# A two-direction chunked scan on four quarters of the TensorE array, with work handed from VectorE and SyncE to GpSimd and ScalarE

## The reference, cut to what matters

```python
def wkv7_scan(r, logw, k, v, a, b, reverse):
    """S_t = S_{t-1} diag(exp(-exp(logw_t))) + (S_{t-1} a_t) b_t^T + v_t k_t^T ;  y_t = S_t r_t"""
    def step(S, inp):
        r_t, w_t, k_t, v_t, a_t, b_t = inp
        sa = jnp.einsum('bhij,bhj->bhi', S, a_t)
        S = (S * w_t[:, :, None, :] + sa[..., :, None] * b_t[..., None, :]
             + v_t[..., :, None] * k_t[..., None, :])
        return S, jnp.einsum('bhij,bhj->bhi', S, r_t)
...
for d, rev in ((0, False), (1, True)):
    wkv = wkv + wkv7_scan(heads(r), heads(logw[:, :, d]), heads(k_d), heads(v),
                          -kk, kk * heads(a_d), rev)
...
c = layer_norm(conv(c) + dw_bias)      # conformer branch, 512 channels
```

## Time and profile before

| what | us |
|---|---|
| median of 3 runs | 2501.82 (2499.22 to 2515.18) |
| profiled execution, its own time | 2509.72 |
| its span, first to last instruction | 2508.0 |
| scan, first level product to the last but four steps | 804.0 to 1112.1: 19 steps |
| last four steps and the end of the scan | 1112.1 to about 1180 |

### The profile page before, as it was taken

One profiled execution on the slowest core, in us unless ns is written; L12 is line 12 of the kernel. 1 busy time (PEld: TensorE's weight loads), 2 busy tenths in 40 slices (PEclk: granted clock), 3 DMA queues, 4 the chain that ended last, 5 costly groups with the idle time before them and its releaser, 6 DMA issues. The chain is left out here.

```text
span 2508.0 us, 50080 instructions
## 1 busy us (share of the span) xinstructions
PE 2328.4 (93%) x19504; PEld 2035.2 (81%) x19504; DVE 1827.3 (73%) x2480; ACT 1208.3 (48%) x1748; POOL 709.5 (28%) x715
## 2 busy tenths in 40 slices
PE   6899999999996999996989896699999999999997
PEld 4788888888876898986767674699999999999996
DVE  5547888988865676675767677677777777777777
ACT  6355454445522334432335332566565666666656
POOL 2234242433412444454453534011011111101111
PEclk9999999999997999998999998799999999999998
DMA  4335253442537766763647352777777777777777
GB/s 151 85 96 162 86 161 116 137 149 87 172 114 226 210 188 188 192 173 79 234 128 258 111 202 101 301 246 256 264 256 245 237 258 255 251 251 260 264 256 245
DMA packets 294772, 479.74 MB, mean 191 GB/s; under 512 B 142224, under 2 KB 209952, under 8 KB 266832
## 3 DMA queue, kind: packets, MB, share of 16 engines
q1 hardware_dynamic: 275552, 412.52, 50.1%
q0 software_dynamic: 7760, 27.08, 4.8%
q10 hardware_dynamic: 11296, 37.82, 4.6%
HBM read 363.51 MB, written 110.69 MB: 189 GB/s over the span
## 5 line engine op out<-in xcount | busy, mean ns | idle before, releaser
L2751 PE MATMUL bank<-e_xt,e_w_high 128*128 128x384 f32 x1792 | 524.7, 357 | 3.7 <-DVE e_xt L2919 2.1
L2906 DVE TENSOR_TENSOR e_w_low<-e_w,e_w_high 128x2048 fp32r<-128x2048 f32 x192 | 436.2, 2284 | 69.2 <-ACT e_w_high L2807 69.2
L2752 PE MATMUL bank<-e_xt,e_w_low 128*128 128x192 f32 x1792 | 449.1, 251 | 0.0
L2807 ACT ACTIVATE e_w_high<-e_w 128x2048 fp32r<-128x2048 f32 x192 | 366.4, 1908 | 107.8 <-PE bank L2773 79.2
L2752 PEld LDWEIGHTS bank<-e_xt,e_w_low 128*128 128x128 f32 x1792 | 342.2, 191 | 0.6
L2751 PEld LDWEIGHTS bank<-e_xt,e_w_high 128*128 128x128 f32 x1792 | 338.1, 189 | 5.5 <-issue 2.5
L462 PE MATMUL bank<-h_high,w_high 128*128 128x512 f32 x864 | 258.0, 407 | 1.5 <-DVE work L872 1.5
L855 DVE SCALAR_TENSOR_TENSOR work<-work,vec 128x1551 f32<-128x1551 f32 x116 | 243.8, 2102 | 2.4
L465 PE MATMUL bank<-h_low,w_high 128*128 128x512 f32 x864 | 244.8, 391 | 0.0
L468 PE MATMUL bank<-h_high,w_low 128*128 128x512 f32 x864 | 243.7, 390 | 0.0
L2685 POOL DMA_INDIRECT xacc_dram<-e_y,e_put x30 | 47.3, 1576 | 651.9 <-DVE e_y L2941 647.3
(11 more groups left out here) (356 smaller groups left out, 5168.7 us busy)
## 6 DMA issues: line engine op xcount, KB each, us to landing
e_w<-in_ew SPq DMA_DIRECT2D x192, 1024.0 KB, 5.9
features_dram<-work SPq DMA_DIRECT2D x48, 512.0 KB, 3.3
fe<-features_dram SPq DMA_DIRECT2D x24, 1024.0 KB, 8.1
x_w<-in_w_mix SPq DMA_DIRECT2D x48, 512.0 KB, 5.1
w<-in_w_in ACTq DMA_DIRECT2D x35, 512.0 KB, 3.6
ba_tok_dram<-work SPq DMA_DIRECT2D x96, 128.0 KB, 2.2
gates_dram<-work ACTq DMA_DIRECT2D x16, 768.0 KB, 4.5
all<-ba_tok_dram SPq DMA_DIRECT2D x96, 128.0 KB, 3.4
```

The costliest lines, as they stand in the source:

```text
L2751: nc.tensor.matmul(*wide, start=(k == 0), stop=False)
L2752: nc.tensor.matmul(*narrow, start=False, stop=False)
L2807: nc.scalar.activation(w_high[n % RING][:], w[n % RING][:], ACT.Copy).then_inc(w_high_done, 1)
L2906: tt(w_low[n % RING][:], w[n % RING][:], w_high[n % RING][:].bitcast(F32), ALU.subtract)\
```

## The change

- The reverse direction is turned over: its factors lie in the other half of the partitions where needed (`HALF`, `TOKEN`, `STATE`), so that its matmuls go from partitions 0-63 to 64-127 and back, through the two other quarters. In `level_n`, `level_x`, `solve`, the products and `products_c` the matmuls of the two directions alternate. `full` and `state` keep their shapes.
- `products` is split. The wide part (64 x 128 outputs, among them G) is made FIRST = 5 steps ahead, the narrow part 4; G's tile ring grows from 5 to 6. `state` of chunk i - 2 now stands at the head of step i.
- `levels` goes from DVE to POOL, in two operations per direction that touch only the blocks that are not zero.
- ACT copies `xx` of the first round in two sides, and where the reverse direction has to change halves, in two pieces of 64 partitions; the same for its `gh`.
- The loads of `st` (`values`) go from SP's list to ACT's. SP loads the reverse `xc` in 3 DMAs instead of 1. Features move up in the list, ahead of inverses and tokens.
- The convolution's additions and multiplications go to POOL, its squares to ACT. The special handling of the last pair's inverses (by halves) is gone.

```diff
-    LEVELS, AHEAD, RING = 2, 4, 5
+    LEVELS, AHEAD, FIRST, RING, RING_ALL, PARTS = 2, 4, 5, 5, 6, 3
+        STATE, TOKEN = ROWS, ROWS[::-1]
+        HALF = [ROWS, ROWS[::-1]]
...
                 for i in range(NCH):
...
-                    if 1 <= i and i + AHEAD - 1 < NCH:
-                        diagonal(i + AHEAD - 1)
-                    if i % 2 == 1 and 3 <= i < NCH - 3:
-                        inverses((i + 1) // 2)
+                    if i + FIRST - 1 < NCH:
+                        diagonal(i + FIRST - 1)
+                    if i % 2 == 0 and 2 <= i < NCH - AHEAD - 2:
+                        features((i + AHEAD + 2) // 2)
+                    if i % 2 == 0 and 2 <= i < NCH - 2:
+                        inverses((i + 2) // 2)
+                    if 1 <= i < NCH - 1:
+                        tokens(i + 1)
...
+                    if 3 <= i < NCH - 1:
                         compact(i + 1)
...
+                    if i + FIRST < NCH:
                         for d in DIRS:
-                            lower(d, i + AHEAD)
-                    if 1 <= i < NCH - 1:
-                        values(i + 1)
...
+                        if d == 0:
+                            sp.dma_start(XC[d][i % 2][:].rearrange("p h x c -> p h (x c)"), src).then_inc(l_x[d][i % 2], 16)
+                        else:
+                            sp.dma_start(XC[d][i % 2][:, :, 0, :], src[:, :, 0:BASE]).then_inc(l_x[d][i % 2], 16)
+                            for out, r in zip(ROWS, HALF[d]):
+                                sp.dma_start(XC[d][i % 2][out, :, 1, :], src[r, :, BASE:2 * BASE])\
+                                  .then_inc(l_x[d][i % 2], 16)
...
+                def level_n(i, n):
                     for hp in L4:
-                        for r in ROWS:
-                            mm = nc.tensor.matmul(t_bank(d)[r, hp, :], NL[d][s][r, n, hp, :], x[d][s][r, hp, 0, :],
-                                                  start=True, stop=True)
+                        for d in DIRS:
+                            for z, r in enumerate(ROWS):
+                                mm = nc.tensor.matmul(t_bank(d)[HALF[d][z], hp, :], NL[d][s][r, n, hp, :],
+                                                      x[d][s][r, hp, 0, :], start=True, stop=True)
...
+                    if i >= 2:
+                        for d in DIRS:
+                            state(d, i - 2)
+                    level_n(i, 0)
                     if post:
-                        for d in DIRS:
-                            solve(d, i - 1)
+                        solve(i - 1)
+                    level_x(i, 0)
+                    if pre:
+                        products_narrow(i + AHEAD)
                     if post:
                         full(0, i - 1)
+                    if i + FIRST < NCH:
+                        products_wide(i + FIRST)
+                    level_n(i, 1)
                     if post:
                         full(1, i - 1)
                     if pre:
+                        products_c(i + AHEAD)
+                    level_x(i, 1)
...
+                def values(d, i):
+                    if i >= 2:
+                        act.wait_ge(m_s[d], i - 1)
+                    rows = slice(chunk_of(d, i) * CH, (chunk_of(d, i) + 1) * CH)
+                    act.dma_start(ST[d][i % 2][TOKEN[d], :, :].rearrange("p h c -> p (h c)"), g.v_tok[rows, :])\
+                       .then_inc(l_v[d][i % 2], 16)
...
                 for i in range(NCH):
+                    if i >= 2:
+                        for d in DIRS:
+                            out(d, i - 2)
+                            store(d, i - 2)
+                            values(d, i)
...
+                def levels(d, i):
+                    if i >= 2:
+                        pool.wait_ge(m_n[d], (i - 1) * LEVELS)
+                    pool.wait_ge(v_g[d], i + 1)
+                    for n, blocks in enumerate((slice(1, None, 2), slice(2, None))):
+                        part = lambda v: v.rearrange("p h (b c) -> p h b c", c=BASE)[:, :, blocks, :]
+                        level = mk("level", n * HD, HD).unsqueeze(1).to_broadcast([P, HP, HD])
+                        ins = tt(part(NL[d][i % 2][:, n, :, :]), part(ALL[d][i % RING_ALL][:, :, G_[d], :]), part(level),
+                                 ALU.mult)
+                    ins.then_inc(p_n[d], 1)
...
                 for i in range(1, NCH - 1):
                     for d in DIRS:
+                        levels(d, i + 1)
+                    for d in DIRS:
                         expand(d, i + 1)
-                    if i % 2 == 0 and i + 4 < NCH:
-                        invert((i + 2) // 2)
+                    if i % 2 == 1 and i + 3 < NCH:
+                        invert((i + 3) // 2)
+                    conv(i)
```

More of the change, by code:

```diff
@@ L1359, in products_c @@
+                def products_c(j):
+                    for d in DIRS:
+                        if j >= AHEAD:
+                            pe.wait_ge(v_t[d], (j - AHEAD) * LEVELS + 2)
+                        elif j >= 1:
+                            pe.wait_ge(v_c[d], j)
+                    u = j // 2 % 2
+                    for hp in L4:
+                        for d in DIRS:
+                            c = inner(d, j)
                             for par, r in enumerate(ROWS):
-                                at = (d * HP + hp) * CH
@@ L1481, in root @@
                                          scale=1.0 / HD).then_inc(f_rooted, 1)
+                for i in range(2):
+                    for d in DIRS:
+                        values(d, i)
                 for j in range(AHEAD):
@@ L1508, in _ @@
                         root()
+                for d in DIRS:
+                    out(d, NCH - 2)
+                    store(d, NCH - 2)
                 for d in DIRS:
@@ L1776, in _ @@
                         summed(0, i - 1)
-                    if pre:
-                        masked(0, i + AHEAD)
-                    for d in DIRS:
-                        level_n(d, i, 1)
-                    if i + 1 < NCH:
-                        levels(1, i + 1)
+                    level_n(i, 1)
                     if post:
```

548 lines of the change are left out of this document (265 added, 283 removed).

## The result

The changed kernel took 2545.45 us (median; 2543.51 to 2554.75), the kernel before 2503.29 on the same chip: a ratio of 1.0170, 95% interval [1.0133, 1.0206]. It is slower by 42 us where 40 us less were forecast, and lies outside the range. The profiled execution has a span of 2543.1 us against 2508.0.

The account below looks back on a forecast made before the run. TensorE was taken as the bound, 15.0 of 16.2 us per step. With 19 steps falling to 14.4 on SP's cycle (34 us) and 6 at the end, 2501.8 - 40 gives 2462 us; range 2418 to 2510.

Parts of the forecast that it names:

- Quarters halve the bursts: TensorE's bursts moved from two quarters to four take half the time: 10.3 us per step becomes 5.1.
- Case 3: Rival: TensorE quarters that share rows do not overlap; PE keeps 15.0 us per step, 2495 to 2505, chance 0.07.
- A burst is paced by the streaming of columns ..., not by the number of instructions: TensorE's bursts: twice the columns take nearly twice the time, 29 to 34 ns for 64 columns.
- SP's own cycle of 14.4: SP's queue of issues and landing waits paces the changed step at 14.4 us, taken between 12.4 and 15.7.
- case 5: Rival: lost cover on SP makes gb loads wait for g_dram; slower, about 2517, up to 2540, chance 0.12.
- Waits that vanish once those are early: SP's queue: its waits for DVE, 18.8 us, and PE, 2.3, in 13.9 steps disappear.
- case 4: Rival: POOL's odd steps of 15.5 us in series with landings, or a falling clock; 2481 to 2502, chance 0.09.
- the two signs that the forecast named for being wrong: Forecast wrong if scan steps come below 13.4 us, or if SP's gb load waits over 3.8.
- Start and end: Scan's start: 0, plus or minus 3 us; its last four steps: 6 us less.

Follow-up runs that it names:

- e6: Kernel before, with state and level-product matmuls each split into two of 32 columns, same columns and results: 1.0293.
- e5: Changed kernel with two heads per matmul in inverse levels, states and narrow products, half of those instructions, wrong results: 1.0101.
- e18: e17 with two heads per matmul in inverse levels, states and narrow products, half of those instructions, wrong results: 2502.58 us, 0.9978.
- e1: Changed kernel with only 1 of 14 rounds kept in each POOL inversion, so incomplete inverses: 1.0107.
- e7: Changed kernel with SP storing the inverses behind the keys and loading xc ahead of the tokens: 1.0079.
- e17: e7 with the diagonal-block loads moved behind the tokens, except in the first three passes: 2520.16 us, 1.0052.

## Why the prediction was wrong

- **Quarters halve the bursts: right, but not for all.** 0.95 us for level_x, as forecast, where the clock is 1.00; `solve` took 1.19 instead of 0.9. Case 3 is out.
- **"A burst is paced by the streaming of columns ..., not by the number of instructions": this step failed.** It was read from bursts in two quarters, where 64-column and 128-column matmuls differ by their columns; 32-column ones, not in the kernel, would have shown the other limit (e6). And a faster burst also asks for more instructions per us: level_x's 64 matmuls, 128 instructions with their weight loads, now start in 0.95 us. The sum had no term for the supply. The stops are 53 us of TensorE's time in the 19 steps; with half the instructions the kernel is 17 to 18.5 us faster (e5, e18), and how much of that comes through the stops no run tells apart.
- **SP's own cycle of 14.4: 14.6 measured, but partly by luck.** The landing of `g_dram` cost 1.9 us per pass, not 3.8 or more, so the lost cover of case 5 did not decide. But the sum took issue times as fixed, and 14.6 holds only as long as SP also stands before the inversion. By the count over 13 passes (from the first keys after 850 us, so the figures differ a little from those above; the own cycle is a pass less the waits for other engines, "gaps" are the short distances between issues):

| us per pass | issues | landings | gaps | own cycle | waits for others |
|---|---|---|---|---|---|
| before | 11.5 | 1.9 | 1.0 | 14.4 | 1.8 |
| after | 11.6 | 1.8 | 1.1 | 14.5 | 3.1 |
| e1 | 14.0 | 1.9 | 1.0 | 17.0 | 0.6 |
| e7 | 13.1 | 2.2 | 1.0 | 16.3 | 0.1 |
| e17 | 14.4 | 0.1 | 1.1 | 15.5 | 0.6 |
| e18 | 13.4 | 0.2 | 1.1 | 14.7 | 0.2 |

  Where the waits for others are all but gone, with all instructions (e1, e7, e17), SP's own cycle is 15.5 to 17.0 us. So the term "I take 14.4" was mis-sized for a kernel in which those waits vanish, and with it the gain of 1.8 us per step. Case 5, 2517 and up to 2540, comes nearest to the result, and its clause on issues that take longer is the part of it that the runs bear out.
- **"Waits that vanish once those are early": this failed.** 1.7 us per pass of waiting for others did not go, they became 2.8: the inversion, whose 11.1 us the forecast had as POOL's load in odd steps (case 4, priced as a small gain and not as a loss), stands ahead of the tokens and `xc` in SP's list. I took SP's cycle and POOL's cycle as two separate maxima, though each waits for the other in every pair. The order of SP's queue is worth 30 us (e17): waits for the inversion, `xc` behind the tokens, and the landing. Neither of the two signs that the forecast named for being wrong came: steps did not fall below 13.4 us on average, and no single wait of SP for `g_dram` was over 2.9 us.
- **The clock.** The inner stretch has 0.85 instead of 0.99. The level fell in the middle of an idle of 6.6 us for `x`, and the bursts from 1061.5 to 1066.0 ran at 0.50, the lower level of 1.2 GHz:

```profile
1061.20 1.13 PE L1249 MATMUL bank<-x,nl 64*64 64x64 f32 x32 [6.61 <-POOL x L1599]
```

```profile
1061.50:1066.00 4.50, 4.50 (x148) 4.50 (x144) 2.04 (x4) 1.88 (x4) 4.50 (x5) 0.50 0.32 57
```

Brought to 0.99, the 234.5 us of PE would be 201, by the estimate above: so up to 33 us of it are the clock, but how much of that lies on the path no run told apart. The step from 1024.9 to 1039.8, with waits of 1.9 and 2.6 us at its two ends, had 1.00.
- **Start and end.** 0 and -6 were forecast, +5.0 and +0.4 measured. The forecast counted four steps in the 45.1 us at the end, where the trace has three. The start was not tested.

In sum: -40 was forecast and +42 measured (+35 in the spans of the profiled executions). The order of SP's queue and half the instructions undo 48 us of these 82, and with that the whole loss. The remaining 34, the gain that was forecast, stay open in part: even e18's steps take 15.5, with the first ones 15.0 to 20.8 us, its start 4.8 us late, its clock 0.89, and SP's single issues longer (203.3 us for 15 passes from 850 to 1076, 13.6 each, against 11.7 in the kernel after), the `xc` pieces behind features above all, one of which took 4.1 us.

## What to carry to other kernels

When a change makes an engine's bursts twice as fast, ask what feeds it at that rate: its instruction stream is a supplier like a DMA, and many small matmuls are where it runs dry. The time of two cyclic lists that wait for each other (SP's loads and POOL's inversion) is not the larger of the two; write down, for each wait in an in-order queue, what stands behind it and who needs that first. And do not book a wait that vanishes as gained: here SP's issues behind 2 MB of features grew by about as much.

## What was not expected of the hardware

- Four quarters of TensorE run together even where two of them share their rows: 15 ns per 64-column matmul with its weight load (level_x, 64 in 0.95 us), 29 in two quarters (64 in 1.86 us).
- Instructions come in pieces of 16 KB, and their queue moved as many in both kernels over the whole span, 1.95 and 1.97 MB. In the 19 steps 59 came before and 58 after, for 385 and 383 matmuls (770 instructions with the weight loads) per step: one per some 250. With 239 matmuls per step 37 came (e5), with 513 it was 77 (e6): again one per some 250, so the queue is TensorE's. The rows of the queues for instructions, 850 to 1076 us, after:

```profile
q8 instruction: 40, 0.66, 1.3%
```

They were never closer than 3.4 us in any of these runs. The stop that ended at 1029.25 ended 2.5 us after a piece started to come (1026.78), and the one that ended at 1051.42 2.3 us after (1049.14).
- Issues just behind a 2 MB load take longer: an `xc` issue took 0.62 us in the median and up to 4.2 just behind features (e17).
